# Gated linear attention in a hybrid decoder layer: block-diagonal queries, compact states and a state update per head

## The reference, cut to what matters

```python
# q, k: 4 heads of 64;  v: 4 heads of 128;  chunks of C tokens
q_t = qc * jnp.exp(bcum)                                  # bcum: cumulative log-decay in the chunk
k_t = kc * jnp.exp(-bcum)
att = jnp.einsum('bhncd,bhnjd->bhncj', q_t, k_t)          # scores inside a chunk
o_intra = jnp.einsum('bhncj,bhnjv->bhncv', jnp.where(tril, att, 0.0), vc)
dS = jnp.einsum('bhncd,bhncv->bhndv', kc * jnp.exp(b_last - bcum), vc)
# state = decay * state + dS, from chunk to chunk
o_inter = jnp.einsum('bhncd,bhndv->bhncv', q_t, s_prev)
o = o_intra + o_inter                                     # then a norm per head and a swish gate
```

## Time and profile before

| | |
|---|---|
| median of 3 runs | 1683.11 us (1680.85 to 1890.51) |
| profiled execution | 1687.72 us, span of its slowest core (core 1) 1686.6 us |
| spans of the 8 cores | 1673.0 to 1686.6 us |
| granted TensorE clock, mean | 0.992 to 0.995 |
| TensorE (PE) busy | 1628.0 us, 97% |
| VectorE busy | 872.0 us, 52% |
| ScalarE busy | 730.4 us, 43% |

### The profile page before, as it was taken

How to read it: one execution, slowest core, us unless ns; L and a number is a source line. 1 busy time by engine, 2 the same in 40 slices (tenths; PEclk the granted TensorE clock), 3 DMA queues, 4 the chain that set the end, 5 groups by cost and what they waited for, 6 DMA issues and landing times.

```text
span 1686.6 us, 24322 instructions; the slowest of 8 cores (1673.0 to 1686.6 us)
## 1 busy us (share of the span) xinstructions
PE 1628.0 (97%) x7859; PEld 753.9 (45%) x7859; DVE 872.0 (52%) x1490; ACT 730.4 (43%) x1182; POOL 120.6 (7%) x228
## 2 busy tenths in 40 slices
PE   6999999998999999999999999999999999999997
PEld 2445444434444444444444444454444444444443
DVE  6662442435765566654565644645645464433336
ACT  5213001046872256952477862268993221210114
POOL 0102011100000000000000000000000011001000
PEclk9999999999999999999999999999999999999999
DMA  9779999898566575555998774886464455623212
GB/s 212 106 114 124 139 125 110 129 148 208 104 146 157 151 154 111 111 130 167 252 207 181 159 192 151 256 220 154 133 192 129 159 157 157 178 70 100 76 38 100
DMA packets 80425, 249.10 MB, mean 148 GB/s; under 512 B 9440, under 2 KB 13808, under 8 KB 79856
## 3 DMA queue, kind: packets, MB, share of 16 engines
q0 software_dynamic: 28864, 107.49, 38.2%
q1 hardware_dynamic: 51440, 140.06, 26.9%
HBM read 282.91 MB, written 54.00 MB: 200 GB/s over the span
## 4 chain that ended last, share of the span: by engine, by line
PE 89%; DMA 4%; DVE 3%; ACT 3%; issue 2%; POOL 0%; DVEq 0%; ACTq 0%; SPq 0%; POOLq 0%
PE ps_all L562 88%; DMA ring<-f1g 2%; ACT mb L588 1%; DVE hS L600 1%; DMA ring<-wb 1%; ACT ma L588 1%; ACT L588 1%; DMA ring<-f2d 1%; DVE ntm L600 0%; DMA hS<-x 0%; DVE mb L595 0%; ACT fa L588 0%; DVE aF L595 0%; DVE gU L600 0%; ACT B L611 0%
## 5 line engine op out<-in xcount | busy, mean ns | idle before, releaser
L562 PE MATMUL ps_all<-ntm,ring 128*128 128x512 bf16 x2224 | 530.5, 381 | 5.1 <-ACT ma L588 2.2
L562 PE MATMUL ps_all<-B,ring 128*128 128x512 bf16 x2016 | 450.4, 379 | 2.8 <-DVE gU L600 1.0
L562 PEld LDWEIGHTS ps_all<-ntm,ring 128*128 128x128 bf16 x2224 | 216.3, 98 | 267.1 <-issue 21.1
L588 ACT ACTIVATE fa<-ps_all 128x512 f32<-128x512 f32 x170 | 101.4, 598 | 468.9 <-PE ps_all L562 460.5
L562 PEld LDWEIGHTS ps_all<-B,ring 128*128 128x128 bf16 x2016 | 195.9, 98 | 237.7 <-issue 8.3
L562 PE MATMUL ps_all<-aF,ring 128*128 128x512 bf16 (+1 forms) x1264 | 294.3, 375 | 3.7 <-DVE hS L600 1.7
L600 DVE SCALAR_TENSOR_TENSOR hS<-ps_all,hS 128x512 f32<-128x512 f32 (+1 forms) x256 | 170.0, 672 | 99.6 <-PE ps_all L562 98.4
L595 DVE TENSOR_TENSOR aF<-fa,ps_all 128x512 bf16<-128x512 f32 x148 | 101.3, 686 | 226.0 <-PE ps_all L562 219.6
L562 PEld LDWEIGHTS ps_all<-aF,ring 128*128 128x128 bf16 x1264 | 123.4, 98 | 147.5 <-issue 10.7
L588 ACT ACTIVATE mb<-ps_all 128x512 bf16<-128x512 f32 (+1 forms) x304 | 161.5, 576 | 39.0 <-PE ps_all L562 36.0
L588 ACT ACTIVATE ma<-ps_all,hv 128x512 f32<-128x512 f32 x104 | 71.2, 687 | 183.1 <-PE ps_all L562 162.2
(11 more groups left out here) (129 smaller groups left out, 1215.1 us busy)
## 6 DMA issues: line engine op xcount, KB each, us to landing
ring<-wb SPq DMA_DIRECT2D x112, 512.0 KB, 4.4
ring<-f1g POOLq DMA_DIRECT2D x44, 512.0 KB, 10.4
ring<-f2bg POOLq DMA_DIRECT2D x44, 512.0 KB, 3.6
wb<-wm POOLq DMA_DIRECT2D x28, 512.0 KB, 14.7
ma<-spill SPq DMA_DIRECT2D x48, 256.0 KB, 5.5
ring<-wb SPq DMA_DIRECT2D x48, 256.0 KB, 3.7
ring<-f2g POOLq DMA_DIRECT2D x22, 512.0 KB, 8.6
f2bg<-ring SPq DMA_DIRECT2D x22, 512.0 KB, 5.5
```

What stands on the lines that cost most here:

```text
L562: i = e.matmul(_ap(o), lhsT=_ap(l), rhs=_ap(r), start=st, stop=sp)
L588: f.add([("act", lambda e: e.activation(out=_ap(out), in_=_ap(in_), func=func, scale=_ap(scale), **kw), c_act(out, bias is not None))], ou ...
```

## The change

1. `ktz` goes. In its place q is written block-diagonal: `qz[pr]` is 128 x 1024, head 0's rows in the first 512 columns, head 1's in the last, zero elsewhere. `u_q` writes it with four DVE operations on 64 rows in place of two on 128; `u_k` loses its four copies.
2. The score group becomes two matmuls of 256 columns, with k of a pair as weights and the block-diagonal q as the moving operand.
3. The update group becomes four matmuls, one per head: 64 weight columns, 128 moving columns; head 0 of a pair writes PSUM partitions 0 to 63 (the first half of the array's columns), head 1 partitions 64 to 127. So `pd`, `gU` and `gS` are 128x128 per pair, and the `blk` mask, its load and its use go.
4. In the output group state x q is one matmul of 256 columns per pair, followed by two of v x scores.
5. The v weights come as two halves of K: 8 K-steps of 128x512 per 128 tokens in place of 16 of 128x256.
6. k stays in its buffer to the last chunk; q takes none from the pool.

```diff
         def u_q():
...
-                stt(st["q"].bf()[:, pr * TT:(pr + 1) * TT], p, 0.125, st["E"][pr], ALU.mult, ALU.mult)
+                for o2 in range(2):
+                    rows = slice(64 * o2, 64 * o2 + 64)
+                    stt(qz[pr][rows, o2 * TT:(o2 + 1) * TT], p[rows, :], 0.125, st["E"][pr][rows, :], ALU.mult, ALU.mult)
...
         def u_k():
...
-                for o2 in range(2):
-                    o = o2 * 64
-                    cp(ktz[pr * 2 + o2][o:o + 64, :], kb[o:o + 64, pr * TT:(pr + 1) * TT], eng="dve", rate=4.0)
...
         def u_v(half):
...
-                mm([(p[:, v * 256:(v + 1) * 256], nM[k][:, i * 128:(i + 1) * 128], st["wv"][v][:, k, :], k == 0, k == 7)
-                    for v in range(2) for k in range(8)])
+                mm([(p, nM[k][:, i * 128:(i + 1) * 128], st["wv"][k // 4][:, k % 4, :], k == 0, k == 7) for k in range(8)])
...
         def u_chunk(i):
...
-            q = [st["q"].bf()[:, pr * TT + i * 128:pr * TT + (i + 1) * 128] for pr in range(2)]
+            q = [qz[pr][:, :].re("p (h n) -> p h n", h=2)[:, :, csl] for pr in range(2)]
+            k = [st["k"].bf()[:, pr * TT + i * 128:pr * TT + (i + 1) * 128] for pr in range(2)]
...
-            mm([(pa[:, h4 * 128:(h4 + 1) * 128], ktz[h4][:, csl], q[h4 // 2], True, True) for h4 in range(4)])
+            mm([(pa[:, pr * 256:(pr + 1) * 256].re("p (h n) -> p h n", h=2), k[pr], q[pr], True, True) for pr in range(2)])
...
-            mm([(pd[:, pr * 256:(pr + 1) * 256], kt[:, pr * 128:(pr + 1) * 128], v[:, pr * 256:(pr + 1) * 256], True, True)
-                for pr in range(2)])
+            mm([(pd[h4 % 2 * 64:h4 % 2 * 64 + 64, h4 // 2 * 128:(h4 // 2 + 1) * 128], kt[:, h4 * 64:(h4 + 1) * 64],
+                 v[:, h4 * 128:(h4 + 1) * 128], True, True) for h4 in range(4)])
...
-            for h4 in range(4):
-                o = po[:, h4 * 128:(h4 + 1) * 128]
-                g.append((o, v[:, h4 * 128:(h4 + 1) * 128], am[:, h4 * 128:(h4 + 1) * 128], True, False))
-                g.append((o, gS[n % 2][h4 // 2][:, (h4 % 2) * 128:(h4 % 2 + 1) * 128], q[h4 // 2], False, True))
+            for pr in range(2):
+                g.append((po[:, pr * 256:(pr + 1) * 256].re("p (h n) -> p h n", h=2), gS[n % 2][pr], q[pr], True, False))
+                for h4 in (2 * pr, 2 * pr + 1):
+                    hsl = slice(h4 * 128, (h4 + 1) * 128)
+                    g.append((po[:, hsl], v[:, hsl], am[:, hsl], False, h4 % 2 == 1))
...
-                stt(gU[pr], gU[pr], gp, pd[:, pr * 256:(pr + 1) * 256], ALU.mult, ALU.add)
-                stt(gS[(n + 1) % 2][pr], gU[pr], gdec[par][pr][:, i:i + 1], blk, ALU.mult, ALU.mult)
+                stt(gU[pr], gU[pr], gp, pd[:, pr * 128:(pr + 1) * 128], ALU.mult, ALU.add)
+                ts(gS[(n + 1) % 2][pr], gU[pr], gdec[par][pr][:, i:i + 1], None, ALU.mult)
```

More of the change, by code:

```diff
@@ L518, in build_program @@
     o_x = [T(ox_h[:, i, :], f"ox{i}") for i in range(4)]
-    ktz = [T(f.sb(f"ktz{i}", [128, TT], BF16)[:], f"ktz{i}") for i in range(4)]
+    qz = [T(f.sb(f"qz{i}", [128, 2 * TT], BF16)[:], f"qz{i}") for i in range(2)]
     vecs = T(f.sb("vecs_s", [128, NV], F32)[:], "vecs")
@@ L528, in build_program @@
     eps_c = T(f.sb("eps_c", [128, 1], F32)[:], "eps_c")
-    gU = [T(f.sb(f"gU{i}", [128, 256], F32)[:], f"gU{i}") for i in range(2)]
-    gS = [[T(f.sb(f"gS{j}_{i}", [128, 256], BF16)[:], f"gS{j}_{i}") for i in range(2)] for j in range(2)]
+    gU = [T(f.sb(f"gU{i}", [128, 128], F32)[:], f"gU{i}") for i in range(2)]
+    gS = [[T(f.sb(f"gS{j}_{i}", [128, 128], BF16)[:], f"gS{j}_{i}") for i in range(2)] for j in range(2)]
     gdec = [[T(f.sb(f"gd{j}_{i}", [128, 4], F32)[:], f"gd{j}_{i}") for i in range(2)] for j in range(2)]
@@ L678, in late_constants @@
             memset(gS[0][i], 0.0)
-        for i in range(4):
-            memset(ktz[i], 0.0)
+        for i in range(2):
+            memset(qz[i], 0.0)
         for kc in range(16):
@@ L1012, in u_kt @@
             cp(st["kt"].bf(), pb, rate=1.9)
-            M2.put(st["k"])
         def u_v(half):
             if half == 0:
-                st["wv"] = [mload("gv", i, 8) for i in range(2)]
+                st["wv"] = [mload("gv", i, 4) for i in range(2)]
                 st["v"] = [M2.get() for _ in range(2)]
@@ L1062, in u_chunk @@
             if i == 3:
-                M2.put(st["q"], st["kt"], *st["v"])
+                M2.put(st["k"], st["kt"], *st["v"])
         def u_x(hh):
@@ L1229, in build_program @@
     f.mark("open")
-    raw_at = [o_mla + [o_gla[:, i, :] for i in range(4)], o_x + ktz]
+    raw_at = [o_mla + [o_gla[:, i, :] for i in range(4)], o_x + [qz[i // 2][:, i % 2 * TT:(i % 2 + 1) * TT] for i in range(4)]]
     raws = []
@@ L1463, in _prep_shared @@
     for i in range(2):
-        block("gv", i, w_in[:, o[5] + i * 256:o[5] + (i + 1) * 256])
+        block("gv", i, w_in[i * 512:(i + 1) * 512, o[5]:o[6]])
         block("gr", i, w_in[:, o[7] + i * 256:o[7] + (i + 1) * 256])
@@ L1482, in _prep_shared @@
     f2g, f2d = ffn_w("ffn2_wg", "ffn2_wu", "ffn2_wd")
-    blk = np.zeros((128, 2, 128), f32)
-    blk[0:64, 0] = 1.0
-    blk[64:128, 1] = 1.0
     smask = np.ones((128, TT), f32)
@@ L1488, in _prep_shared @@
     return {
-        "vecs": vecs, "utri": (jj <= tq).astype(f32), "ident": (jj == tq).astype(f32), "blk": blk.reshape(128, 256),
+        "vecs": vecs, "utri": (jj <= tq).astype(f32), "ident": (jj == tq).astype(f32),
         "smask": smask, "wa2": np.ascontiguousarray(g("gla_w_a2")[0]),
```

5 lines of the change are left out of this document (1 added, 4 removed).

## The result

| | before | changed |
|---|---|---|
| median, runs of all comparisons | 1681.2 us | 1685.84 us |
| ratio, 95% interval | | 1.0028 [1.0021, 1.0035] |
| profiled execution | 1687.72 us | 1690.98 us |
| spans of the 8 cores | 1673.0 to 1686.6 us | 1679.3 to 1689.9 us |

A forecast was written before the change was run, and what follows sets the result against it. TensorE's matmul queue was taken as the bound, busy 1628.0 of 1686.6 us. The sum 1687.7 - 0.4 + 3.0 - 0.7 = 1689.6 us, less the profiled execution's 4.6 us above the median, gave 1685 us, range 1673 to 1699.

The forecast's parts named there:

- Fewer matmuls: v, score and output groups of the mixers: fewer matmuls for the same columns; with the update group's +0.1 us, -0.4 us.
- The change of shape: Update groups in the mixers: entering and leaving the 64-column form costs TensorE 0.19 us, 16 times, +3.0 us.
- rival 1: Update group: the two heads' halves run side by side and no change of shape is paid, 1680 us; chance 0.15.
- The prediction's own test: Update group's starts: about 56 ns apart refutes rival 1, pairs nearly together confirms it, 100 ns or more means rival 2.
- The weight loads: Update group: four weight loads that nothing hides, 98 ns each; with entry and exit at most +9.3 us.
- rival 2: Update group: four unhidden weight loads plus entry and exit make the kernel slower, 1691 us; chance 0.15.
- DVE's steps: State update in the mixers: shorter `gU` and `gS` pieces in the chain, -0.7 us, at most -2.4 us.
- DVE's work: DVE in the mixers: 6 to 14 us less work net, worth nothing by itself since DVE idles 43% there.
- q's bank: Mixers: a second read-out holds a q bank 0.69 us more, 8 times; taken as nothing, at worst +5.5 us.
- The new order: Scheduler decides anew from the mixers on: TensorE's pauses there change by 10 us either way, nothing in the middle.
- Rival 3: Mixers: the new order halves TensorE's pauses, 1675 us; chance 0.13.
- Rival 4: Mixers: the new order pauses more, above all with q's banks held longer, 1695 us; chance 0.13.

## Why the prediction was right or wrong

**The forecast** of no change beyond 2% held, and the bound was read rightly: a queue that holds 1597.9 us of matmuls gains only where columns go, and this change removes none. That 1685.84 us came so near 1685.0 is luck in part. The forecast went out from 1683.1, the median of three runs; from the 1681.2 of all runs the same sum gives 1683.1. The change was put at +1.9 us and was +4.7.

**Fewer matmuls,** -0.4 us: v's matmuls are 216 ns apart, as put. The -0.4 itself is too small for any of the times; v alone measured 0.9996 [0.9985, 1.0006].

**The change of shape,** +3.0 us: right in kind and place. The start 0.09 us late is what the decay projection in the earlier trace rows had shown. It was mis-sized: 0.11 us per group over the old 218 ns and not 0.19, and 1.3 us in all and not 3.1, since in some groups it falls together with a wait. What I had left out is that entering and leaving is paid and, at the same time, the pairs run side by side: four matmuls in an estimated 139 ns (84 + 55) where I took 224. I had put the two as alternatives, the forecast and rival 1. The prediction's own test for this, pairs that start nearly together, came out for rival 1, the late start for the forecast; both are true.

**The weight loads** (rival 2): wrong in size. The four loads of 64 columns overlap and take 0.14 us together, and the second pair starts 80 ns behind the first; nowhere do 98 ns each add up. Whether the loads have a part in the late start or in the 80 ns wasn't tested.

**DVE's steps:** `gU` 343 ns (0.37 forecast), `gS` 284 ns (0.12 to 0.37). `gU` left the chain, and TensorE's waits for it, 1.1 us in the profile before, are gone. But the -0.7 us doesn't appear in the mixers' pauses, which rose. **DVE's work** fell by 2.0 us where I had 6 to 14. The steps of GLA are lighter by what the sum says (4.6 us of copies gone, -3.9 by `gU`, -6.3 by `gS`, +5.5 by q: -9.3). Most of it was filled up. Read-out copies may go to DVE or ScalarE, and the rows of copies and casts on DVE sum to 51.6 us where they summed to 49.1 with 4.6 us of `ktz` copies among them: 7.1 us of others came over from ScalarE, and -9.3 + 7.1 = -2.2 is near the 2.0 measured. The step that failed here is that I took the assignment as given.

**q's bank,** 0 (up to +5.5 us): no wait of TensorE for a q read-out stands in its waits, and the read-outs themselves ran with 0.6 us of idle before all 16.

**The new order,** 0 ± 10 us: +3 to +4 us. It is what is left of the loss, 4.7 + 0.4 - 1.3 = 3.8 us, the larger part, and the experiments show its kind: with the changed instructions three orders gave 1.0028 to 1.0064, with those of before three gave 1.0000 to 1.0091. The whole loss of this change lies within what a cost that means nothing can do. But the orders of each kind have the opening's wait in common, the short one or the long one, so 1.4 us of the 3.8, and the low clock behind it, is no draw among them: it comes with this change each time. I had put the order as new "from the mixers on" and the raw tiles of the opening, moved from `ktz` to `qz`, at no price. That term was put at nothing without a reason. Rival 3 (less pauses) is wrong. Rival 4 has the sign right, its size a third, and its cause, q's banks, wrong.

What stays open: why the opening's order changed. The program keeps dependencies by tile, and two raw tiles now share one `qz` where each had a `ktz` of its own; that may be the reason, but no experiment was aimed at it. And some 2 us of the mixers' new pauses were not traced to single waits.

## What to carry to other kernels

Matmuls in column halves have a fare for getting in and out. Here it was about 190 ns, against 32 ns saved with each pair of 128 columns: an estimated six pairs in a row before it pays, if the 80 ns of a pair hold in a longer row, and this kernel has two at a time, sixteen times. Where the array is the bound and the columns stay the same, fewer matmuls are worth some 2.4 ns each, and the lighter steps of DVE, which idled, brought nothing that the times show.

Behind a list scheduler, any edit is two edits, the instructions and a new order, and here the second was worth up to 15 us of 1682 by itself. The new order needn't begin where the edited code does: compare all of it, the opening too. Before a few tenths of a per cent are credited to an edit, pin its price and look whether the order stayed, or measure three or four orders of each. A long run of steps with a late deadline ahead of the one that the bound engine waits for is what to look for, above all where no filling work is left.

## What the runs showed of the hardware

Two matmuls with 64 weight columns each, writing different halves of the PSUM partitions, start 4 ns apart, and the next pair 80 ns after the first, where one of 128 columns in the whole array takes 56 ns. So even side by side a pair is not as fast as one matmul (80 against 56 ns), only faster than two (112). The group started 93 ns late both in the changed kernel and in the kernel before with this one edit.

DVE takes as long for 64 rows as for 128 also in small operations (345 and 343 ns for 128 columns in f32). `gS`, as a TENSOR_SCALAR with 128 columns, took 284 ns, 59% of the 482 ns that four times the columns took the earlier trace rows: most of a small operation is not its columns.

TensorE's granted clock has two levels in these traces, and a wait for another engine can cost more than its length. Behind a pause of 2.7 us in the opening, 40 of 54 cores ran the next 4 to 8 matmuls of 512 columns 0.43 us apart (1.2 GHz) and not 0.216 (2.4 GHz), some 0.9 to 1.7 us more. Behind the pause of 1.3 us at the same place none of 30 did. The mean clock of the whole span, 0.99 in both kernels, doesn't show it.
